# Score products of a chunked gated scan: full 128x128 products against 32x32 blocks in column groups

## What is computed

```python
b = jnp.cumsum(gc, axis=2)                       # log of the forget gates
rel = jnp.where(causal, b[:, :, :, None, :] - b[:, :, None, :, :], -jnp.inf)
A = jnp.einsum('bhtc,bhsc,bhtsc->bhts', qc, kc, jnp.exp(rel))      # the scores
o = einsum('bhts,bhsv->bhtv', A, vc) + einsum('bhtc,bhcv->bhtv', qc * jnp.exp(b), S)
S_new = exp(b_last)[..., None] * S + einsum('bhsc,bhsv->bhcv', kc * jnp.exp(b_last - b), vc)
```

## Time and profile before

| what | us |
|---|---|
| median of 3 runs | 1182.93 (1182.42 to 1189.31) |
| the profiled execution, span from first to last instruction | 1181.6 |
| PE busy / PEld busy / DVE busy / ACT busy | 1150.4 / 1078.0 / 641.1 / 507.0 |

### The profile page before, as it was taken

One profiled execution on the slowest core, in us unless ns is written; L12 is line 12 of the kernel. 1 busy time (PEld: TensorE's weight loads), 2 busy tenths in 40 slices (PEclk: granted clock), 3 DMA queues, 4 the chain that ended last, 5 costly groups with the idle time before them and its releaser, 6 DMA issues.

```text
span 1181.6 us, 23304 instructions
## 1 busy us (share of the span) xinstructions
PE 1150.4 (97%) x9669; PEld 1078.0 (91%) x9669; DVE 641.1 (54%) x1239; ACT 507.0 (43%) x1026; POOL 148.4 (13%) x156
## 2 busy tenths in 40 slices
PE   8999999999999999989999799999999999999998
PEld 6799998989898989878999799999999999998998
DVE  4767585766666665756342752463355246526432
ACT  4643344444444434353111553654356346437221
POOL 1000000001010100000000171063025204500000
PEclk9999999999999999989999899999999999999999
DMA  9863525253435253415321537522742472352531
GB/s 330 281 182 97 158 73 168 69 163 93 148 93 163 90 161 94 130 54 177 112 83 54 164 92 171 132 76 57 167 125 68 105 179 76 92 130 74 169 102 52
DMA packets 232143, 147.78 MB, mean 125 GB/s; under 512 B 7811, under 2 KB 226013, under 8 KB 231526
## 3 DMA queue, kind: packets, MB, share of 16 engines
q1 hardware_dynamic: 217392, 134.40, 39.5%
q10 hardware_dynamic: 14646, 11.89, 3.0%
HBM read 124.23 MB, written 22.02 MB: 124 GB/s over the span
## 4 chain that ended last, share of the span: by engine, by line
PE 92%; DVE 3%; DMA 2%; ACT 1%; SPq 1%; issue 1%; DVEq 0%; ACTq 0%
PE PJ L378 25%; PE PJ L1540 17%; PE PJ L1255 14%; PE PJ L399 9%; PE X L1111 5%; PE PJ L425 2%; PE X L1233 1%; PE X L1656 1%; PE X L1137 1%; PE X L1151 1%; PE PJ L1565 1%; PE X L1621 1%; PE X L1683 1%; PE PJ L622 1%; DMA pre<-in_ada_w_dram 1%; PE X L1235 1%
## 5 line engine op out<-in xcount | busy, mean ns | idle before, releaser
L351 DVE TENSOR_TENSOR w_lo<-raw,w_hi 128x1024 fp32r<-128x1024 f32 (+1 forms) x128 | 156.8, 1238 | 172.3 <-ACT w_hi L343 171.6
L343 ACT ACTIVATE w_hi<-raw 128x1024 fp32r<-128x1024 f32 (+1 forms) x128 | 129.1, 1024 | 156.4 <-PE PJ L1540 73.1
L1540 PE MATMUL PJ<-w_hi,h_hi 128*128 128x256 f32 x600 | 167.6, 287 | 0.8 <-DVE w_lo L351 0.7
L1540 PE MATMUL PJ<-w_lo,h_hi 128*128 128x256 f32 x600 | 164.6, 283 | 0.0
L378 PE MATMUL PJ<-h_hi,w_hi 128*128 128x288 f32 (+1 forms) x736 | 161.5, 301 | 0.1
L378 PE MATMUL PJ<-h_hi,w_lo 128*128 128x288 f32 (+1 forms) x736 | 157.7, 296 | 0.0
L378 PE MATMUL PJ<-h_lo,w_hi 128*128 128x288 f32 (+1 forms) x736 | 157.4, 295 | 0.0
L1540 PE MATMUL PJ<-w_hi,h_lo 128*128 128x256 f32 x480 | 135.8, 283 | 0.0
L378 PEld LDWEIGHTS PJ<-h_hi,w_hi 128*128 128x128 f32 x736 | 118.1, 189 | 4.7 <-issue 3.7
L378 PEld LDWEIGHTS PJ<-h_hi,w_lo 128*128 128x128 f32 x736 | 118.9, 189 | 0.0
L378 PEld LDWEIGHTS PJ<-h_lo,w_hi 128*128 128x128 f32 x736 | 118.8, 189 | 0.0
(11 more groups left out here) (324 smaller groups left out, 2252.6 us busy)
## 6 DMA issues: line engine op xcount, KB each, us to landing
raw<-in_a_w_in_dram SPq DMA_DIRECT2D x48, 512.0 KB, 4.1
raw<-in_ada_w_dram SPq DMA_DIRECT2D x32, 512.0 KB, 3.7
raw<-in_b_w_in_dram SPq DMA_DIRECT2D x64, 256.0 KB, 3.6
kvc<-in_cache_kv_w_dram SPq DMA_DIRECT2D x24, 512.0 KB, 5.5
pre<-in_ada_w_dram SPq DMA_DIRECT2D x16, 512.0 KB, 9.9
s<-in_state_hgrn_dram SPq DMA_DIRECT2D x8, 1024.0 KB, 7.1
out_hgrn_sample_dram<-s ACTq DMA_DIRECT2D x8, 1024.0 KB, 5.0
raw<-in_a_w_out_dram SPq DMA_DIRECT2D x16, 512.0 KB, 4.5
```

The costliest lines, as they stand in the source:

```text
L343: act.activation(w_hi[:, i % SPLITS, 0:size], raw[:, n % RAWS, 0:size], ACT.Copy).then_inc(hi_done, 1)
L351: dve.tensor_tensor(w_lo[:, i % SPLITS, 0:size], raw[:, n % RAWS, 0:size], w_hi[:, i % SPLITS, 0:size].bitcast(F32), ALU.subtract).then_in ...
L1540: last = pe.matmul(PJ[:, tile // 2, tile % 2 * 256:tile % 2 * 256 + 256], a, b[:, k, :], start=(first and k == 0 and i == 0), stop=(kk == ...
```

## The change

- Levels 0 to 5 are made as four 32x32 blocks on the diagonal of each chunk. Block q of a chunk goes to PSUM partitions 32q to 32q + 31, so the four blocks lie in four 32-column groups of the array; all are written at the same 32 columns of the bank, and a chunk's level is 128 partitions x 32 columns. The samples are a fifth chunk with 4 blocks (each of its two 32-token blocks made twice), in levels 0 to 3.
- Three levels fit in one bank (3 x 160 columns): levels 0 to 2 in bank 0, 3 to 5 in bank 1 (`gram_at`), 6 and 7 in bank 2 (`wide_at`). The semaphores `gram_ready` and `gram_read` count three groups a head, not eight levels. TensorE doesn't wait for reads between levels any more.
- Groups 0 and 1 are issued together ahead of the row tiles, group 2 behind tile 0. VectorE reads groups 0 and 1 before the running sum and group 2 at i = 3.
- VectorE gathers levels 0 to 5 in `atd` (128 x 5 x 32) by masks of 32 columns and spreads it into `at` by four copies of 32x128 (`at` is set to zero once, ahead of the loop); levels 6 and 7 are copied as before. The sample product takes its weights from `atd`, as two products of 32x32 tiles.

```diff
@@ constants
-    s, t = np.arange(P)[:, None], np.arange(P)[None, :]
+    s, t = np.arange(P)[:, None] % BL, np.arange(BL)[None, :]
...
-    out["c_levels"] = np.stack(masks, 1).astype(np.float32).reshape(P, -1)
+    out["c_levels"] = np.stack([*masks, s == t], 1).astype(np.float32).reshape(P, -1)
@@ dve_level
-                    dve.wait_ge(gram_ready, 8 * (h - 1) + i + 2)
+                    dve.wait_ge(gram_ready, 3 * (h - 1) + (i + 1) // 3 + 1)
@@ dve_gram
+        def gram_at(i):
+
+            return X[:, i // 3, i % 3 * NB * BL:(i % 3 + 1) * NB * BL].rearrange("p (n t) -> p n t", t=BL)
+
+        def dve_gram(dve, chain, g, group):
+
+            dve.wait_ge(gram_ready, 3 * g + group + 1)
+            if group == 0:
+                if g >= 1:
+                    dve.wait_ge(orow_ready, g)
+                chain(dve.tensor_tensor(atd[:], gram_at(0), eye[:].unsqueeze(1).to_broadcast([P, NB, BL]), ALU.mult))
+            if group < 2:
+                for i in range(max(3 * group, 1), 3 * group + 3):
+                    n = NB if i <= 3 else CH
+                    ins = dve.copy_predicated(atd[:, 0:n], lev[:, i - 1, :].unsqueeze(1).to_broadcast([P, n, BL]),
+                                              gram_at(i)[:, 0:n])
+                    if i % 3 < 2:
+                        chain(ins)
             else:
...
+                if g >= 1:
+                    dve.wait_ge(op_ready, g)
+                for q in range(4):
+                    r = slice(BL * q, BL * q + BL)
+                    dve.tensor_copy(at[r, :, r], atd[r, 0:CH])
+                for i in (6, 7):
+                    for s0_, s1_, t0_, t1_ in level_blocks(i):
+                        ins = dve.tensor_copy(at[s0_:s1_, :, t0_:t1_], wide_at(i)[s0_:s1_])
             ins.then_inc(gram_read, 1)
-            dve.wait_ge(gram_read, 8 * g + i + 1)
+            dve.wait_ge(gram_read, 3 * g + group + 1)
@@ dve_step
-                    gram()
+                    if i == 3:
+                        gram()
@@ pe_grams
+        def pe_grams(pe, g, group):
             b = g % 2
...
+            if group == 0:
+                pe.wait_ge(k_done, g + 1)
+                wait_read(pe, ticket_w(g, 0))
+                if g >= 1:
+                    pe.wait_ge(ms_read, g)
+            if group == 2 and g >= 1:
+                pe.wait_ge(fin_done, 2 * g)
+            for i in range(3 * group, min(3 * group + 3, 8)):
                 pe.wait_ge(lv_done, XS * g + i)
...
+                left, right = (k_[:, b], q_[:, b]) if i == 0 else (qk[:, i - 1], qk[:, i - 1])
+                if i < 6:
+                    for n in range(NB if i <= 3 else CH):
+                        for q in range(4):
+                            t = n * P + BL * q if n < CH else TP + BL * (q % 2)
+                            last = pe.matmul(gram_at(i)[BL * q:BL * q + BL, n], left[:, t:t + BL], right[:, t:t + BL],
+                                             start=True, stop=True)
...
+            last.then_inc(gram_ready, 1)
@@ pe_states
-            pe.wait_ge(gram_read, 8 * g + 8)
+            pe.wait_ge(gram_read, 3 * g + 3)
...
-            pe.matmul(X[0:TS, 2, 0:ADV], ats[:], v_[0:TS, b, CH, :], start=True, stop=False)
+            for x in range(2):
+                r = slice(BL * x, BL * x + BL)
+                pe.matmul(X[r, 2, 0:ADV], atd[r, CH, :], v_[r, b, CH, :], start=True, stop=False)
@@ pe_step
...
                 def between(tile):
-                    grams(tile + 1)
+                    if tile == 0:
+                        grams(2)
...
-                grams(0)
+                grams(0, 1)
...
             elif h == AH:
-                for n in range(4):
-                    grams(n)
+                grams(0, 1, 2)
@@ vector, ahead of the loop
-            chain(dve.tensor_copy(lev[:].rearrange("p l t -> p (l t)"), lev_raw))
+            dve.memset(at[:], 0.0)
+            dve.tensor_copy(eye[:], lev_raw[:, MASKED * BL:])
+            chain(dve.tensor_copy(lev[:].rearrange("p l t -> p (l t)"), lev_raw[:, 0:MASKED * BL]))
```

More of the change, by code:

```diff
@@ L33 @@
 MASKED = 5
+BL = 32
+NB = CH + 1
 XS = 8
@@ L741, in program @@
         st = ExitStack()
-        lev = sb("lev", [P, MASKED, P], U8, stack=st)
+        lev = sb("lev", [P, MASKED, BL], U8, stack=st)
+        eye = sb("eye", [P, BL], stack=st)
         reset = sb("reset", [P, T], stack=st)
@@ L756, in program @@
         at = sb("at", [P, CH, P], stack=st)
-        ats = sb("ats", [TS, TS], stack=st)
+        atd = sb("atd", [P, NB, BL], stack=st)
         qk = sb("qk", [P, len(LEVELS), T], stack=st)
@@ L770, in program @@
         cond.close()
-        lev_raw = oz_flat[:, 5 * D:5 * D + MASKED * P]
+        lev_raw = oz_flat[:, 5 * D:5 * D + (MASKED + 1) * BL]
         st1 = ExitStack()
@@ L900, in act_step @@
                 act.activation(sq0[:, :, TP:T], os_[:], ACT.Square).then_inc(sq_done, 1)
[L903 to L919, removed]
-            else:
-                ins = dve.copy_predicated(at[:], lev[:, i - 1, :].unsqueeze(1).to_broadcast([P, CH, P]), src)
+        def gram_at(i):
+            return X[:, i // 3, i % 3 * NB * BL:(i % 3 + 1) * NB * BL].rearrange("p (n t) -> p n t", t=BL)
@@ L989, in dve_step @@
                 dve.tensor_scalar(k_[:, b], fg[:], -1.0, 1.0, ALU.mult, ALU.add).then_inc(k_done, 1)
-            grams = iter(range(8 if scan else 0))
+            grams = iter(range(3 if scan else 0))
             def gram():
@@ L1021, in dve_step @@
                         dve_level(dve, h, i - 1)
-            for _ in range(8):
+            if scan and not new:
                 gram()
-            if scan and not new:
                 oz_lo(0, 2)
@@ L1083, in level_blocks, with wide_at @@
         def level_blocks(i):
-            if i < 6:
-                return ((0, P, 0, P),)
             L = LEVELS[i - 1]
             return tuple((x, x + L, x + L, x + 2 * L) for x in range(0, P, 2 * L))
-        def pe_grams(pe, g, levels):
+        def wide_at(i):
+            L, c0 = LEVELS[i - 1], (i - 6) * CH * BL
+            return X[:, 2, c0:c0 + CH * L].rearrange("p (c t) -> p c t", c=CH)
+        def pe_grams(pe, g, group):
             b = g % 2
-            for i in levels:
-                pe.wait_ge(lv_done, XS * g + i)
[L1094 to L1113, removed]
@@ new lines, in pe_grams @@
+            if group == 0:
[6 more added lines that the diff above has]
+            for i in range(3 * group, min(3 * group + 3, 8)):
+                pe.wait_ge(lv_done, XS * g + i)
+                left, right = (k_[:, b], q_[:, b]) if i == 0 else (qk[:, i - 1], qk[:, i - 1])
[5 more added lines that the diff above has]
+                                             start=True, stop=True)
+                else:
+                    for c in range(CH):
+                        for s0_, s1_, t0_, t1_ in level_blocks(i):
+                            last = pe.matmul(wide_at(i)[s0_:s1_, c], left[:, c * P + s0_:c * P + s1_],
+                                             right[:, c * P + t0_:c * P + t1_], start=True, stop=True)
@@ L1184, in pe_step, with grams @@
                 project_T(ticket_w(h, 1), ("w", h, 1))
-            def grams(n):
-                if scan and n < 4:
-                    pe_grams(pe, g, (2 * n, 2 * n + 1))
+            def grams(*groups):
+                for n in groups if scan else ():
+                    pe_grams(pe, g, n)
             keys = [("w", h, 2), ("w", h, 3)]
```

## The result

The changed kernel takes 1166.55 us (median of 4 runs, 1163.78 to 1168.57) where the kernel before takes 1183.41 in the same series; the ratio is 0.9836, 95% interval 0.9812 to 0.9860. Forecast were 1148.5 us and 1142 to 1162. The direction was right, half of the gain is missing. The profiled execution spans 1163.8 us, 17.8 less than the 1181.6 of before.

A forecast was written before the change was run, and what follows sets the result against it. TensorE was taken to bound seven of eight head steps, VectorE the last. Savings of 7 x 4.2 + 5 = 34.4 us from 1182.9 gave 1148.5 us, range 1142 to 1162.

The forecast's parts named there:

- the sum of a full step: TensorE, levels 0 to 5 in a full step: 1.8 us products, edges about 0.09 and 0.1, waits 0.2; sum 2.2 us.
- rival 3: Levels 0 to 5: instructions arrive only at 0.053 us a record; slower than before, 1224 us; chance 0.04.
- 0.008 forecast: TensorE, levels 0 to 5: each of 224 small records in four column groups takes 0.008 us.
- 4.08 saved for 4.2: TensorE, score products of a full step: 7.51 us become 3.3, saving 4.2 us a step.
- rival 1: Levels 0 to 5: only two of four groups overlap, 0.016 us a record; kernel 1161 us; chance 0.14.
- rival 2: Levels 0 to 5: a floor between records wherever they go, 0.023 us each; kernel 1172 us; chance 0.08.
- my 175.0: VectorE in a full step: masked keys made from 174.3 to 175.0, before TensorE needs them at 175.8.
- 330 forecast: VectorE: a masked copy over 160 columns takes 0.33 us.
- all reads of a head 4.0 us (4.2): VectorE: a head's reads of the products shrink from about 6.3 us to 4.2 us.
- My smallest margin: VectorE's schedule in a full step: everything is in time for TensorE, the tightest by 0.8 us.
- The last head: Step h = 8, without projections: VectorE's reads end 7 us earlier, 2 taken off for lower clock; 5 us saved.
- The idle PE and the clock: Last head: TensorE idles from about 515.5 to 520.0, and the state products behind may meet the lower clock.

The follow-up runs named there:

- the keys moved: The changed kernel with VectorE making the masked keys at i = 5 instead of i = 6, runs of products not split: 1166.03 us (one run).
- two-group run: The changed kernel with the order of the small products turned so that neighbours alternate between two column groups: 1169.55 us (one run).
- split: The changed kernel with product group 1 issued behind tile 0 and group 2 behind tile 1: 1157.21 us, ratio 0.9749 to the kernel before.
- the split and early keys: Split, with VectorE making the masked keys at i = 5 instead of i = 6: 1153.19 us, ratio 0.9710 to the kernel before.

## Why the prediction was wrong

**The step that failed** is the sum of a full step: "Sum 2.2 us", with rival 3 set aside on a chance of 0.04. Rival 3 named the right thing, the instruction supply, and priced it wrongly: as an even 0.053 us a record that decides from 0.028 on. The sum had nothing for it. The runs show no slow rate. Delivery goes in blocks of 256 and only the time between two borders counts. Inside a block the array got 0.0086 us a record; at a second border 1.1 us after the first it stood up to 2.7 us. So a case between the forecast and "slower than before" was missing, and it was the real one: about 10.2 us of stops over seven heads by the table.

**The records.** 0.008 forecast, 0.0086 measured; the run of 224 took 1.93 us, with the edges near the 2.2. From a head's first product to the state products (L1137 before, L1153 after) the kernel before took 23.89 us, and 19.81 where neither stops nor keys held it (head 4 with the keys moved): 4.08 saved for 4.2, and 4.18 without the stop of 0.11 us that head 4 still has. The two-group run at 0.0114 also refutes rival 1's 0.016, and rival 2's floor of 0.023 is not there once neighbours lie in different groups. Nor is the floor of 25 ns from start to start of the Trainium skill, page "TensorE: Matmul & The Clock Gate", section "Wait — 56ns, not 53.3ns?": 8.6 ns were measured.

**The clock.** I had no loss of clock in steps 1 to 7. The stops brought it: after two of the four longest (2.67 and 2.10 us idle) the granted clock was 0.50 for 3.4 us, 1.5 us lost each; after the other two (2.24 and 2.08) it stayed at 1.00. With the split the steps of heads 0 to 5 had none.

**VectorE's schedule.** The masked copy of 160 columns took 341 ns (330 forecast), all reads of a head 4.0 us (4.2). But the masked keys were ready 1.5 us later than my 175.0 (470.97 in head 6's step, 176.5 on the scale of the forecast). 1.1 of that is the subtraction stretched beside GpSimd. It costs 0.3 us where there is no stop (head 4), 0.4 in each step of split. My smallest margin was 0.8 us, and I had taken VectorE's durations as fixed though they depend on what runs beside them.

**The last head.** 5 us saved forecast, bounds 3 and 8. From its first product to ScalarE's last low part of the head (L1270 before, L1286 after, just ahead of a table load): 36.87 us before, 31.78 after, 5.09 saved. The idle PE and the clock behave as forecast. A piece of PE's timeline (in brackets the idle time ahead of it and its releaser):

```profile
505.54 1.12 PE L1135 MATMUL X<-ident,kh 128*128 128x128 f32 x4 [3.49 <-DVE at L932]
```

The window of the changed kernel from 504.00 to 510.80 (columns as above):

```profile
504.00:510.80 6.80, 5.26 (x28) 2.62 (x29) 5.19 (x12) 1.96 (x4) 0.00 (x0) 0.50 0.01 4
```

**The rest of the kernel**, which nobody touched, took 1.55 us more (632.92 before from that low part on, 634.47 after). It contains a half-clock stretch at 1067.2 to 1070.6 that the profiled execution of before lacks. That this stretch is the 1.55 us fits the numbers (3.4 us at half clock) and was not shown.

In sum: 7 x (4.08 - 0.09) = 27.9 of 29.4 us were there; 0.09 is nearly all what the rest of a step grew by. Some 13.5 were given back between first product and state products: stops 10.2 inside and 0.4 behind a run, clock 3.0, keys 0.6 (heads 4 and 6), together 14.2, less 7 x 0.1, since the 19.81 that I measure against holds head 4's stop. Last head -5.1, rest +1.6, start +0.1: 17.8.

## What to carry to other kernels

When many small products replace few large ones, price the delivery of instructions as blocks, not as a rate: here the 256 instructions between two borders must last longer than 3.2 to 3.8 us, or the array stops at the second, inside the run or just behind it. Break such a run into pieces with long operations between them; splitting it in two won back some 9 us (1166.55 to 1157.21, in two series), though it costs 0.2 to 0.3 us of switches a step (57.28 with the split and early keys, 57.10 for head 4 without the split, a stop of 0.11 included). And when the bound engine gets faster, look at the next engine's durations beside its new neighbours, not at those of the old schedule.

## What the runs showed of the hardware

- PE's small products in four column groups start every 0.0086 us on average, each with a weight load of its own; two groups give 0.0114, one 0.0213 (0.032 for the first seven, until other records are pulled forward).
- Instructions come 16 KB at a time (256 instructions, 0.9 to 1.6 us of transfer in the changed kernel). Where PE stood waiting, it went on 1.3 to 1.5 us after the end of a transfer. Equal loop bodies take different times (57.38 to 61.19 us) by where they lie against these blocks, and 64 instructions added elsewhere in the program move the loss from one head to another.
- PE's matmuls don't always start in program order: in head 6 the first record of level 1 starts at 451.00, the last two of level 0 at 451.01 and 451.03.
- A VectorE subtraction of 0.45 us took 1.54 us beside a GpSimd product of 1.51 us, and ended 0.3 us after it, as did one of 0.77 us in the kernel before.
